# A gap of 64 bytes in place of 32 between the weight rings and the streamed tiles

## The reference

```
h = x
h = h + hybrid_mixer(rmsnorm(h), w_in [1024 x 7712], ..., w_up_ssd, w_up_gla, w_o)
h = h + mem_cross_attention(rmsnorm(h), rmsnorm(mem), w_xq, w_xkv, w_xo)
h = h + (silu(g) * u) @ w_ffn_out          # g, u = split(rmsnorm(h) @ w_ffn_in), width 2816
h = rmsnorm(h)
h = concat(meta_tokens, h)                 # 272 tokens
h = h + stick_breaking_mixer(rms_norm(h), w_qkv, w_o)
h = h + relu(rms_norm(h) @ up0)**2 @ down0 # width 4096
h = h + rglru_mixer(rms_norm(h), w_in, conv, gates, w_out)
h = h + relu(rms_norm(h) @ up1)**2 @ down1 # width 4096
return rms_norm(h)[:, 16:]
```

## Time and profile before

| | |
|---|---|
| runs | 1178.45 us median, 1178.0 to 1180.21 |
| profiled execution | 1178.66 us, of which the span from the first to the last instruction is 1176.8 us |
| TensorE busy | 1163.9 us (99%), 9580 matmuls |
| TensorE weight load busy | 1142.1 us (97%) |
| VectorE / ScalarE / GpSimd busy | 839.9 us (71%) / 680.0 us (58%) / 37.8 us (3%) |
| granted TensorE clock | 0.997 of full speed |
| HBM | 195.45 MB read, 167 GB/s over the span |

### The profile page before, as it was taken

One profiled execution on the slowest core, in us unless ns is written; L12 is line 12 of the kernel. 1 busy time (PEld: TensorE's weight loads), 2 busy tenths in 40 slices (PEclk: granted clock), 3 DMA queues, 4 the chain that ended last, 5 costly groups with the idle time before them and its releaser, 6 DMA issues.

```text
span 1176.8 us, 25252 instructions
## 1 busy us (share of the span) xinstructions
PE 1163.9 (99%) x9580; PEld 1142.1 (97%) x9580; DVE 839.9 (71%) x1257; ACT 680.0 (58%) x1029; POOL 37.8 (3%) x60
## 2 busy tenths in 40 slices
PE   9999999999999999999999999999999999999997
PEld 8999889999999999999999999999999999999997
DVE  6998767987856877776667748666545898776453
ACT  6755547656535666655556637656444777665442
POOL 2002311100000000000000000000000000000000
PEclk9999999999999999999999999999999999999998
DMA  6655434576553566656543326555665545666661
GB/s 226 189 173 177 127 108 143 173 223 188 161 170 114 173 199 190 187 189 185 181 148 119 122 72 206 175 177 184 194 183 174 147 154 165 207 186 187 189 191 59
DMA packets 56775, 197.52 MB, mean 168 GB/s; under 512 B 7152, under 2 KB 9456, under 8 KB 56576
## 3 DMA queue, kind: packets, MB, share of 16 engines
q1 hardware_dynamic: 54480, 193.68, 53.4%
q10 hardware_dynamic: 2224, 2.84, 0.8%
HBM read 195.45 MB, written 1.05 MB: 167 GB/s over the span
## 4 chain that ended last, share of the span: by engine, by line
PE 85%; DVE 8%; ACT 4%; issue 2%; DMA 1%; DVEq 0%; SPq 0%; ACTq 0%
PE acc L474 14%; PE acc L475 14%; PE acc L480 14%; PE acc L468 11%; PE acc L470 11%; PE acc L469 11%; DVE wlo L1655 3%; PE acc L533 1%; PE acc L537 1%; PE acc L534 1%; ACT whi L1148 1%; PE mix L807 1%; PE mix L788 1%; DVE softp L2152 1%; DVE sp L2142 1%
## 5 line engine op out<-in xcount | busy, mean ns | idle before, releaser
L1655 DVE TENSOR_TENSOR wlo<-raw,whi 128x1024 fp32r<-128x1024 f32 x366 | 448.1, 1227 | 179.8 <-ACT whi L1148 179.6
L1148 ACT ACTIVATE whi<-raw 128x1024 fp32r<-128x1024 f32 x366 | 385.7, 1059 | 321.2 <-PE acc L480 163.0
L474 PE MATMUL acc<-xh,whi 128*128 128x256 f32 (+1 forms) x1448 | 359.0, 286 | 0.0
L475 PE MATMUL acc<-xl,whi 128*128 128x256 f32 (+1 forms) x1448 | 353.9, 282 | 0.0
L474 PEld LDWEIGHTS acc<-xh,whi 128*128 128x128 f32 x1448 | 271.8, 188 | 4.3 <-issue 3.0
L475 PEld LDWEIGHTS acc<-xl,whi 128*128 128x128 f32 x1448 | 272.6, 188 | 0.3
L480 PE MATMUL acc<-xh,wlo 128*128 128x256 f32 (+1 forms) x1448 | 202.3, 282 | 0.0
L470 PE MATMUL acc<-hh,wlo 128*128 128x256 f32 (+1 forms) x688 | 194.4, 283 | 0.0
L468 PE MATMUL acc<-hh,whi 128*128 128x256 f32 (+1 forms) x688 | 194.3, 282 | 0.0
L469 PE MATMUL acc<-hl,whi 128*128 128x256 f32 (+1 forms) x688 | 194.1, 282 | 0.0
L480 PEld LDWEIGHTS acc<-xh,wlo 128*128 128x128 f32 x1448 | 185.0, 188 | 0.0
(11 more groups left out here) (397 smaller groups left out, 1571.3 us busy)
## 6 DMA issues: line engine op xcount, KB each, us to landing
raw<-w SPq DMA_DIRECT2D x366, 512.0 KB, 3.7
hT<-xT SPq DMA_DIRECT2D x2, 512.0 KB, 6.6
mem<-memT ACTq DMA_DIRECT2D x1, 1024.0 KB, 6.4
rgw<-w ACTq DMA_DIRECT2D x2, 512.0 KB, 5.2
out<-hT SPq DMA_DIRECT2D x4, 128.0 KB, 2.5
out<-hT ACTq DMA_DIRECT2D x4, 128.0 KB, 2.8
xdt<-wsmall SPq DMA_DIRECT2D x1, 192.0 KB, 7.3
pr<-par ACTq DMA_DIRECT2D x1, 114.0 KB, 4.4
```

The lines of the kernel that those rows point to most:

```text
L474: nc.tensor.matmul(dst, whi[:, slot, n, :], rh, start=first, stop=False)
L475: nc.tensor.matmul(dst, whi[:, slot, n, :], rl, start=False, stop=False)
L1148: act.activation(whi[:, j, :, :].rearrange("p k c -> p (k c)"), raw[:, j, :], ACT.Copy)\
L1655: dve.tensor_tensor(wlo[:, j, :, :].rearrange("p k c -> p (k c)"), raw[:, j, :], whi[:, j, :, :].rearrange("p k c -> p (k c)").bitcast(F32 ...
```

## The change

The unused tile `between` grows from 32 to 64 bytes, and everything behind it up to `small` moves up by 32 bytes. `small` shrinks by 32 bytes (its last eight columns are not used), so all tiles behind it stay where they were. The packed rows of `hh` and `hl` get a `skip` of 8 elements, 32 bytes.

```diff
-        sb("between", [P, 8])
+        sb("between", [P, 16])
...
-        small = sb("small", [P, 88])
+        small = sb("small", [P, 80])
...
         xh1, xl1, yh1, yl1, hh1, hl1 = [packed(tile, skip) for tile, skip in
-                                        ((xh, 128), (xl, 0), (yh, 128), (yl, 0), (hh, 0), (hl, 0))]
+                                        ((xh, 128), (xl, 0), (yh, 128), (yl, 0), (hh, 8), (hl, 8))]
```

## The result

The changed kernel takes 1182.07 us (median of 8 runs, 1181.77 to 1183.53), against 1178.45 us for the kernel before on the same chip (8 runs, 1178.0 to 1180.21). The ratio is 1.0031, with a 95% interval of 1.002 to 1.0042: slower by 3.6 us, a little beyond what counts as no change. The profiled execution took 1183.26 us with a span of 1181.4 us, 4.6 us more than the one before, so it lies 1.2 us above the median.

A forecast was written before the change was run, and what follows sets the result against it. TensorE bounds the kernel: number of matmuls times the distance between their starts. All parts were taken as 0, sum 0 against the profiled 1178.66 us, 0.2 above the median; forecast 1178.5 us, range 1171 to 1188 us, forecast's own 1176 to 1181.

The forecast's parts named there:

- the slower rival: Packed phases: distance 64 makes streams meet the weight load, +0.6 to +1.5 ns per matmul, 1182 to 1189 us; chance 0.35.
- the prediction's own last sign: Packed phases: prediction is wrong if their pace changes by more than 0.45 ns in either direction.
- The bound: Whole kernel: time is the number of TensorE matmuls times the distance between their starts, plus small pieces.
- steps 4 and 5: Shifted tiles on VectorE and ScalarE, 0.1 us either way; first DMAs into `hT`, 0, bounds -0.5 to +0.5 us.
- step 5: First DMAs into `hT`, now landing on a multiple of 64: taken as 0, bounds -0.5 to +0.5 us.
- Step 1: Packed rows of x, y and hidden layers, distance 32 to 64, 5496 matmuls: pace stays 116.7 ns, change 0.
- Step 2: 272-token rows of x and y, and the gate, 1920 matmuls: taken as 0, bounds -2.5 to +2.5 us.
- Step 3: Unchanged distances, 768 matmuls of `hh` with 272 tokens and 192 of the memory: change 0.
- The control: `hh` with 272 tokens, 830 to 900 us, must stay at 561 matmuls in any case.
- the first window: Packed phase at 470 to 520 us: 431 matmuls if the forecast is right, 426 to 429 if the slower rival is.
- The faster rival: Kernel gets faster than forecast, chance 0.23; its place, mechanism and size are not in the text given.
- The change does what it says: Opposes a rival that the 32 bytes never reach TensorE's pace; that rival shares the forecast's time, no separate chance given.

The follow-up runs named there:

- the map: Kernel before, gap 32 bytes, packed rows of x, y, hh moved by skips to other distances, four runs: 1192.05, 1175.83, 1187.27 and 1191.43 us, one execution each.
- the run with the gap alone: Against the kernel before: `between` grown to 64 bytes, all packed rows brought back to distance 32 by skips; 1179.0 us, ratio 1.0.
- the run with the moved rings: Against the kernel before: weight rings, gap, x, y and packed hh moved 32 bytes together, their distances kept; 1179.87 us, ratio 1.0008.
- The push at the entry: Changed kernel plus one unread matmul in the first units of ffi and up1; 1177.35 us, ratio 0.9993; repeated 1182.13 us, ratio 1.0018.

## Why the prediction was right or wrong

The range held the time by its width, since it had been made wide enough for both rivals, and the forecast itself missed: 1182.07 lies 1.3 us above its upper edge, 1180.8. The sign is that of the slower rival (0.35), and the time lies at that rival's lower end. By the prediction's own last sign, a pace that changes by more than 0.45 ns, it was wrong.

- *The bound.* Right: the difference is TensorE's busy time, and the 3.6 us by which the medians differ lie in the distance between starts. The further 1.1 us of the profiled execution are its lower clock from 9 to 12 us. VectorE, ScalarE and the first DMA stayed, as steps 4 and 5 had it; the latter two are shown by the rows above, not by an experiment of their own. The 0.5 us that step 5 allows either way is the author's estimate and no run shows it; the DMA was on the path for 6.13 in place of 6.14 us.
- *Step 1, packed rows, is the step that failed.* It took the value of distance 32 for distance 64, "the nearest row". The long phases measured +1.1 ns, within the +1.5 that it allowed from above. That 32 and 288 bytes gave one pace said nothing on 64: the map shows 5 ns between places 16 bytes apart, so no row is near another in this. Its reading of the gate, that 1.1 ns more shows the place of the rows, was not safe either: its own window of y holds the gate's pace, 117.8, at distance 32. The sum by the measured pace, 5496 x 1.1 = 6.0 us, is more than the 3.6 us lost in all from 18.3 us on. The 192 matmuls of y behind the cross attention were at 117.8 before as well, and the first mixer got quicker by 0.9 us, with x in part at 113.3 and with the values by token at 113.5 ns. For these the sum had no term, though their distance changed too.
- *Step 2, rows of 272 tokens.* Taken at 0 with bounds of 2.5 us either way; up0 measures 0.30 us, 0.4 ns for a matmul, a unit of the gate takes 2.84 in place of 2.83 us, and the run with the gap alone shows no difference in time. The mean over a turn of four does have a preferred start, a slight one.
- *Step 3.* The control held: 561 matmuls in its window, 97.97 us.
- *The slower rival.* Its price, 0.6 to 1.5 ns per packed matmul, holds the 1.1 of the long phases; the first window counts 427, within its 426 to 429. Its mechanism, the meeting of the streams with the weight load, fits what the run with the moved rings and the pace beside idle and busy copies showed. That 116.7 belongs to distance 32 alone is not so: upg held it at 208. Its remark that a phase can fall into a slower pace and keep it was the main thing in the trace, at 380 to 396 us; it should have been a forecast of its own. That window is at 117.8 also in the changed kernel, where the distance is 64. The narrow products, 116.7 ns at every distance, were the case against this rival. They had weight loads of 121 in place of 188 ns; whether that is why they misled, no run shows.
- *The faster rival.* It got 0.23, less than the slower one, because the trace before holds no pace below 116.7. No run shows the term from which its time, and with it the lower side of the range, was worked out; it was the author's estimate. What the runs show in its place is 113.3 ns, 3.3 less: at distance 64, in the first mixer of the changed kernel and in ffo with `hh` alone at 64, and at 192 in four long phases at once. That rows start on multiples of 64 is not enough for it: in the run with moved rings they do, at 116.7. The values by token, with 118.2 the slowest streams of 256 columns before, went to 113.5, although the addresses that stream stayed and only the loaded tokens moved.
- The change does what it says: at distance 64 the packed rows do behave otherwise.

What stays open: why 64 and 192 allow 113.3, and what chooses between the two paces of a phase. The push at the entry did not settle the second; its two traces show that the instructions and addresses alone do not settle it.

## What to carry to other kernels

Where TensorE streams back to back, compute the distance between the starts of the streamed rows and of the weight blocks and sweep it in small steps, by a skip inside the tile rather than by the layout: here the best place was worth 0.8% (1167.61 us, ratio 0.9922), and the worst cost 1.05% (1192.05 against 1179.64 us, one execution). Read the result by phase from the count of matmuls in a fixed window, not from the total, since one phase can gain what another loses. A steady pace can be one of two, so look at all single times; look at the granted clock of the first microseconds before two profiled executions are compared; and do not take the pace at one address for that at the next.

## What the runs showed of the hardware that was not expected

- In these traces, float32r matmuls with 256 columns run at a few steady distances between starts, the same within 0.02 ns in different phases: 113.3, 116.7, 117.8, 120.0 ns among them (ffi lasts 118.05 us in four kernels and 119.16 or 119.17 in five others).
- The pace depends on where the streamed row lies to the weights being loaded (the memory's keys, which stayed, went from 116.7 to 120.0 ns when the rings moved), with differences between neighbours 16 bytes apart (64: 113.3 or 117.8; 80: 118.3 or 120.0). It holds with the roles exchanged: where weights stream and tokens are loaded, 118.2 ns became 113.5.
- A phase keeps its pace over a thousand matmuls (ffi: 1056), and the next phase at the same distance had the same one in every trace (ffi and ffo, up1 and dn1). Phases in front can change it without a change to its own operands (ffi at 192: 113.3 ns, or 117.8 with y at 32), and so can something that differs between executions of one program (y at 64 behind the recurrent mixer: 113.3 and 117.8).
- The same program shows groups of times some 5 to 7 us apart (1167.5 and 1172 to 1174; 1173 and 1180; 1175 to 1178 and 1182).
